# Gate products as seven block products for eight, with sums on GpSimd and additions on VectorE

## The reference

```python
h = x * (1 + sc1) + sh1
# three branches of attention: a (differential), b (neighbourhood), c (grouped queries)
ga, gb, gc = jnp.split(jax.nn.sigmoid(h @ w_gate_l + b_gate_l), N_BRANCH, axis=-1)
y = (ga * (oa @ w_br_l[0]) + gb * (ob @ w_br_l[1]) + gc * (oc @ w_br_l[2])) @ w_o_l
x = _layernorm(alpha * x + g1 * y, ln_g_l[0], ln_b_l[0])
h2 = x * (1.0 + sc2) + sh2
m = _moe(h2, w_router, router_bias, moe_w1_l, moe_w3_l, moe_w2_l)   # 16 experts, 2 taken
x = _layernorm(alpha * x + g2 * m, ln_g_l[1], ln_b_l[1])
```

## Time and profile before

| what | value |
| --- | --- |
| runs, us | 2165.38, 2165.5, 2169.61; median 2165.5 |
| span of the profiled execution, us | 2168.7 |
| PE busy, us | 2054.0 (95%) |
| DVE busy, us | 1131.9 (52%) |
| ACT busy, us | 508.2 (23%) |
| GpSimd busy, us | 196.2 (9%) |
| PE, products of 128x320, records of hT by ring | 2048, busy 604.0 us |
| mean granted clock of PE | 0.982 of full speed |

### The profile page before, as it was taken

The page is one execution under the profiler, slowest core; times in us unless marked ns, Lnnn a source line. Parts: engine busy times, 40 slices in busy tenths (PEclk is TensorE's granted clock), DMA queues, the critical chain, the costliest instruction groups (busy, mean ns, idle before and its releaser), DMA issues. The chain is left out here.

```text
span 2168.7 us, 25186 instructions
## 1 busy us (share of the span) xinstructions
PE 2054.0 (95%) x9738; PEld 1212.0 (56%) x9738; DVE 1131.9 (52%) x1782; ACT 508.2 (23%) x1007; POOL 196.2 (9%) x234
## 2 busy tenths in 40 slices
PE   7999999999999999699899999999999999969996
PEld 3457766576467654344244676656755676434432
DVE  1135458343447765756342453764534444866664
ACT  2014300242134400122130342003412342002221
POOL 1000010020110000100120002001101000010003
PEclk9999999999999999899999999999999999989997
DMA  7311146411122161689771112562111114238996
GB/s 303 129 47 39 37 144 237 138 54 44 39 81 98 68 278 75 252 342 359 265 256 39 63 35 69 199 214 86 47 53 49 42 40 172 91 136 313 382 350 186
DMA packets 62681, 317.01 MB, mean 146 GB/s; under 512 B 14824, under 2 KB 15280, under 8 KB 34272
## 3 DMA queue, kind: packets, MB, share of 16 engines
q1 hardware_dynamic: 32688, 232.41, 28.6%
q0 software_dynamic: 13136, 53.64, 7.6%
q10 hardware_dynamic: 16736, 29.32, 3.8%
HBM read 286.70 MB, written 27.07 MB: 145 GB/s over the span
## 5 line engine op out<-in xcount | busy, mean ns | idle before, releaser
L1081 PE MATMUL ps<-hT,ring 128*128 128x320 f32 x2048 | 604.0, 438 | 0.0
L1081 PEld LDWEIGHTS ps<-hT,ring 128*128 128x128 f32 x2048 | 369.7, 190 | 138.3 <-issue 3.3
L1081 PE MATMUL ps<-ring,hT 128*128 128x512 f32 (+1 forms) x960 | 386.6, 558 | 2.5 <-DVE hT L1995 1.7
L1081 PE MATMUL ps<-ring,zT 128*128 128x512 f32 (+2 forms) x992 | 317.6, 600 | 2.0 <-ACT zT L1898 2.0
L1081 PEld LDWEIGHTS ps<-ring,hT 128*128 128x128 f32 x960 | 178.8, 190 | 184.0 <-issue 174.8
L1081 PE MATMUL ps<-R,ring 128*128 128x512 f32 (+1 forms) x768 | 211.1, 435 | 4.6 <-DVE zT L2267 3.2
L1081 PEld LDWEIGHTS ps<-ring,zT 128*128 128x128 f32 (+2 forms) x992 | 121.5, 156 | 149.1 <-issue 146.3
L1830 ACT COPY R<-ps 128x512 f32<-128x512 f32 (+2 forms) x170 | 96.1, 565 | 374.7 <-PE ps L1330 372.5
L1081 PEld LDWEIGHTS ps<-R,ring 128*128 128x128 f32 x768 | 116.9, 191 | 99.3 <-issue 93.1
L2112 DVE SCALAR_TENSOR_TENSOR R<-ring,cs,R 128x2048 f32<-128x2048 f32 x56 | 131.7, 2352 | 5.5 <-DMA ring<-in_wall 3.5
L2193 DVE RECIPROCAL rinv<-rsum 128x2 f32<-128x2 f32 x96 | 15.9, 166 | 224.6 <-ACT R L1816 224.6
(11 more groups left out here) (302 smaller groups left out, 2045.7 us busy)
## 6 DMA issues: line engine op xcount, KB each, us to landing
ring<-in_wall SPq DMA_DIRECT2D x188, 1024.0 KB, 6.1
hT<-in_wall SPq DMA_DIRECT2D x20, 1024.0 KB, 8.5
y_all<-R ACTq DMA_DIRECT2D x27, 512.0 KB, 7.0
R<-in_wall SPq DMA_DIRECT2D x10, 1024.0 KB, 9.2
R<-in_rows POOLq DMA_DIRECT2D x2, 4096.0 KB, 15.7
R<-mrows POOLq DMA_DIRECT2D x16, 512.0 KB, 19.2
R<-in_x ACTq DMA_DIRECT2D x10, 512.0 KB, 9.5
h_rows<-R ACTq DMA_DIRECT2D x10, 512.0 KB, 2.6
```

Source lines behind the costliest of these rows:

```text
L1081: ins = nc.tensor.matmul(out, w, m, start=start, stop=stop, **kw)
```

## The change

A gate piece is now worked on as 2 x 2 blocks (`pair` p): rows low and high (four `k` each), columns first and second 128, by 2 x 2 blocks of tokens (low and high rows, early and late 320). Seven products of blocks (`LOW_LOW` to `HIGH_HIGH`), each of four 128x128x320 products (`STEPS`), take the place of eight. For this

- GpSimd makes sums of tokens (`token_sum`, 128 x 1280 columns, four a branch, of which branch 2 reuses three) and for each pair four sums of weights of 128x512 (`first_sums`, `last_sum`). The token sums of branch 0 lie in `SG`, those of branches 1 and 2 mostly in ring slots 4 and 5, so that only four slots hold weights there. The output weights ("o") wait for the last gate product.
- ACT copies the first product (`LOW_LOW`), takes tanh of the third straight from PSUM (`HIGH_LOW` is summed on top of `LOW_LOW`), and tanh of the other three quarters from `sg`.
- DVE makes six additions of 128x320 a pair into `sg` (`add_products`), called behind the maximum and behind the finish of each slot.
- PE waits for these at each product's first step.
- The slots have three steps ahead of the transpositions in place of four (branches 0 and 1), and a branch has 112 steps in place of 128. In branch 2 slots 1 to 16 have (3, 2) for (3, 3), slot 0 eight for four, and the tail 8 and 4 for 8 and 8.
- `masked_bias` of branch 1 is interleaved with the sums slot by slot.

The diff, cut to its core:

```diff
-TAIL_FILL = (8, 0, 8)
+TAIL_FILL = ((8,), (), (8, 4))
 UNIT_FILL = 2
 FILL = (
-    ((0, 6, 0),) + 6 * ((0, 4, 3),) + 4 * ((0, 4, 2),) + 6 * ((0, 4, 3),) + ((0, 6, 0),),
-    ((4, 6, 0),) + 16 * ((0, 4, 3),) + ((0, 6, 0),),
-    ((0, 4, 0),) + 16 * ((0, 3, 3),) + ((0, 4, 0),),
+    ((0, 6, 0),) + 12 * ((0, 3, 3),) + 4 * ((0, 3, 2),) + ((0, 6, 0),),
+    ((4, 6, 0),) + 16 * ((0, 3, 3),) + ((0, 6, 0),),
+    ((0, 8, 0),) + 16 * ((0, 3, 2),) + ((0, 4, 0),),
 )
...
+KEPT_SLOTS = (4, 5)
+TURNS = (2, 3, 0, 1)
...
+    w = j - len(PROJECT_SLOTS)
+    if w < 0:
+        at = PROJECT_SLOTS[j]
+    elif w < n:
+        at = TURNS[w % 4]
+    else:
+        at = (*KEPT_SLOTS, TURNS[n % 4], TURNS[(n + 1) % 4], TURNS[(n + 2) % 4], TURNS[(n + 3) % 4])[w - n]
...
+                        if what == ("o", 0, 0):
+                            sp.wait_ge(pe_gate, gate_no(2, PAIRS - 1, HIGH_HIGH))
                         load(i, lay, WALL.index(what))
...
+                    def first_sums(br, p):
+
+                        i, w = gate_piece(br, p)
+                        pool.wait_ge(full[slot_of(layer, i)], 16 * loads_by(layer, i))
+                        if br or p:
+                            pool.wait_ge(pe_gate, gate_no(br, p, LOW_LOW) - SEVEN + LATE)
+                        ch.step(nc.gpsimd.tensor_tensor(part_sum, w[:, low, 128:256], w[:, high, 128:256], ALU.add), g_sum)
+                        ch.step(nc.gpsimd.tensor_tensor(cross_sum[:], part_sum, w[:, low, 0:128], ALU.subtract), g_sum)
+                        ch.step(nc.gpsimd.tensor_tensor(w[:, low, 128:256], w[:, low, 0:128], w[:, low, 128:256], ALU.subtract), g_sum)
+
+                    def last_sum(br, p):
+
+                        i, w = gate_piece(br, p)
+                        pool.wait_ge(pe_gate, gate_no(br, p, CROSS))
+                        ch.step(nc.gpsimd.tensor_tensor(cross_sum[:], w[:, high, 0:128], cross_sum[:], ALU.subtract), g_sum)
...
+                            if c == 7:
+                                gate_sums(2, 0)
                             if c in (6, 7):
                                 for t in range(NT):
...
+                        for s in range(ITEMS + 2):
+                            if s:
+                                gate_sums(br, products_by(br, min(s, SLOT_COUNT) - 1, 2))
...
+                            if o == LOW_LOW:
+                                if k == 0:
+                                    if br or p:
+                                        pe.wait_ge(v_part, adds_by(br, p, LOW_LOW) - 1)
...
+                                weights, tokens = w[:, k, 0:128], hT[:, k, 0:320]
+                            elif o == CROSS:
+                                if k == 0:
+                                    if br or p:
+                                        pe.wait_ge(v_part, adds_by(br, p, LOW_LOW))
+                                    pe.wait_ge(g_sum, SUMS * (PAIRS * br + p) + 2)
+                                    pe.wait_ge(g_tok, sums_ready(br, 1))
+                                weights, tokens = cross_sum[:, k, :], token_row(layer, br, 1, k)
...
+                            elif o == DOWN:
+                                if k == 0:
+                                    pe.wait_ge(v_part, adds_by(br, p, CROSS))
...
+                            ins = mm(ps[:, 6 + (SEVEN * p + o) % 2, 0:320], weights, tokens, k == 0 and o != HIGH_LOW, k == STEPS - 1,
+                                     frees=k < STEPS - 1, skip_group_check=o in (LOW_LOW, HIGH_LOW))
...
+                            dve.wait_ge(pe_gate, gate_no(br, p, o))
+                            got = ps[:, 6 + (SEVEN * p + o) % 2, 0:320]
+                            first, second, third_, fourth = quarters(br, p)
+                            if o == CROSS:
+                                dve.wait_ge(a_low, PAIRS * br + p + 1)
+                                ch.step(V_.tensor_tensor(fourth, fourth, got, ALU.add), v_part)
+                            elif o == DOWN:
+                                ch.step(V_.tensor_tensor(third_, fourth, got, ALU.add), v_part)
+                            elif o == ACROSS:
+                                ch.step(V_.tensor_tensor(second, fourth, got, ALU.add), v_part)
+                                ch.step(V_.tensor_tensor(fourth, third_, got, ALU.add), v_part)
+                            elif o == LATE:
+                                ch.step(V_.tensor_tensor(second, second, got, ALU.add), v_part)
+                            else:
+                                ch.step(V_.tensor_tensor(third_, third_, got, ALU.subtract), v_part)
...
+                            if s == 0:
+                                add_products(br, fills(br)[0] // STEPS)
                             if s < ITEMS:
                                 maxima(br, s)
+                                if s:
+                                    add_products(br, products_by(br, s, 1))
...
                                 norm_output(done)
+                            if s < SLOT_COUNT:
+                                add_products(br, products_by(br, s, 2))
                             if br == 2 and not last_layer and 1 <= s < ITEMS:
                                 next_partials(s)
```

More of the change, by code:

```diff
@@ L219, in slot_of @@
         return SLOT_MOE[layer][i - MOE_FIRST[layer]]
[L220 to L225 removed]
+    return RING_ORDER[layer][place_in_ring(layer, i)]
 def summed_by_dve(layer, i):
@@ L961, in _ @@
                                     powers(small[:, 8:8 + nh], small[:, 0:nh])
+                            if c == 7:
+                                gate_sums(2, CROSS + 1)
+                            if c == 5:
+                                n = pieces.index((layer, ("in", 4, 1)))
+                                pool.wait_ge(freed, taken_by(layer, n)[1])
+                                for j in range(4):
+                                    token_sum(1, j)
+                                pool.wait_ge(mrow_out, 16 * 2 * STRIPS)
+                                gate_sums(1, 0)
                             i = PU.index((br, c, CTX))
@@ L1234, in project @@
                         done = len([q for q in QU if PU[q][0] <= br])
-                        for q in range(done - LAST_QK[br], done):
-                            fill(br, TAIL_FILL[br])
+                        for q, n in zip(range(done - LAST_QK[br], done), TAIL_FILL[br] or (0,) * LAST_QK[br]):
+                            fill(br, n)
                             transpose_unit(q)
@@ L1255, in fill @@
[L1255 to L1257 removed]
+                            p, step = divmod(filled[0] - PAIRS * SEVEN * STEPS * br, SEVEN * STEPS)
+                            o, k = divmod(step, STEPS)
+                            w = take("gate", ahead).rearrange("p (k n) -> p k n", k=8)
```

245 lines of the change are left out of this document (186 added, 59 removed).

## The result

The changed kernel takes 2174.9 us (median of 12 runs, 2167.3 to 2182.2), the kernel before 2169.2 (12 runs beside them). The ratio is 1.0029, with a 95% interval of 1.0016 to 1.0042: 0.3% slower, where 1.3% faster was forecast. The profiled execution's span is 2171.4 us, its mean granted clock 0.976 (0.982 before).

The account below looks back on a forecast made before the run. PE was taken as the bound nearly everywhere, VectorE level in branch 2, layer 0. Gains 9.8 + 14.0 + 6.5 - 1.8 - 1.0 = 27.5 us gave 2141.2, or 2138.0 on the median's scale; range 2130 to 2146, 8-in-10 2118 to 2157.

Parts of the forecast that it names:

- What bounds the kernel: Whole kernel: TensorE is busy 2054.0 of 2168.7 us; a removed step saves 0.54 us where PE sets the slot's length.
- Branch 0, slots 3, 7 and 11, waits of 0.9, 1.4, 0.9: Branch 0 attention: PE waits there for additions behind an output's norming, cutting a gain of 8.1 to 4.9 us a layer.
- rival B: GpSimd sums and VectorE hinder each other, in branch 2 of layer 0 and branch 0's outputs: about 2153 us; chance 0.20.
- Branch 1, slot 1, 1.07 later: Branch 1, slot 1: fourth product waits for an addition behind item 0's finish, 1.07 us later; branch net gain 7.0 a layer.
- Branch 2, slot 0 and 1: Branch 2, tail to slot 1, both layers: +2.1 for an addition behind the finish, -2.7 for five fewer steps; about 0.1 gained.
- Projection, chunk 6 to 7, 0.5 a layer: Branch 2 projection: weight sums delay GpSimd's power and chunk 7's unit, PE waits 0.4 to 0.5 us, 1.0 in both layers.
- Branch 2 of layer 0, 4.5 longer in its attention: Branch 2, layer 0: VectorE's 7.10 us loop lengthens; attention 116.3 us against 111.8 before, net 1.8 lost in the sum.
- The 2.6 us for additions behind the finish: Branch 2, layer 0: two additions in slot 4 and one each in slots 5, 9 and 13 lengthen VectorE's loop, 2.6 us.
- Ring of four, 0: Weight slots: two of six hold token sums, output weights wait; taken as 0, or 4 us lost if pieces came 5 later.
- A: Waits at product boundaries and VectorE's bound in layer 0 are smaller than worked out: gain 41, 2124.6 us; chance 0.15.
- C: VectorE's hand-over is late at every one of 168 products, PE waits 87 us: slower, 2201 us; chance 0.07.
- D: Weight pieces come late through the ring of four, 1.1 us for each of 24 gate pieces: 2165 us; chance 0.08.

Follow-up runs that it names:

- work in the wait: The changed kernel with two unused 128x320 products ahead of each of the three longest-waiting product starts, in both layers: 2161.3 us, ratio to before 0.9962.
- sums clear: The changed kernel with only GpSimd's order altered, sums waiting for VectorE's units at chunk 7 and output norming in branch 0: 2156.3 us, ratio 0.9943.
- idle sums: The kernel before the change with GpSimd making 96 sums of a scratch tile nobody reads, placed like the change's weight sums: 2180.3 us, ratio 1.0041.
- sums short: The changed kernel with GpSimd's sums cut to 4 columns of each block, waits, products and additions kept, output wrong: 2147.2 us.
- both orders: The changed kernel with VectorE's additions moved earlier and GpSimd's sums held until VectorE's unit or norming is done: 2138.8 us, ratio 0.9868.

## Why the prediction was wrong, point by point

- **What bounds the kernel**: right. PE sets the pace, and every plain slot fell by what was forecast.
- **Branch 0, slots 3, 7 and 11, waits of 0.9, 1.4, 0.9**: slots 7 and 11 were right (1.2 and 0.7), slot 3 failed: 2.83. The failed step is that the norming was taken at its length in the trace of before, 0.69 twice, though rival B had it listed as of the kind that collides. Two held-up operations are 1.9 us; the half speed behind them 1.7 and 3.0 more (11.55 and 12.76 against 9.8 with work in the wait, which has the same additions). Slot 15 holds the same collision with a pair's last sum (L2260 at 1.64, slot 7.17 for 6.25, and 6.29 with the sums clear). Together with a tenth each in slots 7 and 11 and 0.24 in slot 13 that is the shortfall of 11.6 in both layers.
- **Branch 1, slot 1, 1.07 later**: the mechanism and its size were right. The product waited for the addition behind the finish; shifted by the 1.33 us by which the branch started later, it started at 421.42 (422.75 less 1.33), and 420.83 + 0.52 = 421.35 was forecast. What failed is the end of the working: that behind the wait PE goes on at its pace. It ran at half speed, 1.5 and 1.8 us more. The rest of 6.1 is in slots 9, 10 and 13 (1.3 a layer).
- **Branch 2, slot 0 and 1**: the same step failed: behind the wait PE was taken to go on at its pace. The wait was there, 2.65 long, and the half speed behind it cost 1.6 to 1.7; the work beside a sum (L2420) another 0.36. In layer 1 this is the shortfall of 3.3, but for slots 6 and 7 (0.97, the output's copy behind the additions), which no term had.
- **Projection, chunk 6 to 7, 0.5 a layer**: mis-sized. I had the unit of chunk 7 late by its power. The unit of chunk 6 came first: its two operations were held up by 1.1 and 0.9, PE waited 3.82 in place of 1.79, and the clock fell. It cost 4.3 a layer. 3.7 of this the sums clear give back (121.25 to 117.55), and the idle sums show it apart from the change.
- **Branch 2 of layer 0, 4.5 longer in its attention**: 10.0 longer. 2.0 are the start, as above. The rest is slots 6, 7, 10 and 14 (9.91, 7.91, 8.98, 7.94). In slot 6 the output's copy stands behind two additions and a modulation sum that a sum of GpSimd holds up (3.10 for 2.35), PE waits 2.63 and goes on at half speed:

```profile
678.64 3.10 DVE L2366 SCALAR_TENSOR_TENSOR R<-ring,cs,R 128x2048 f32<-128x2048 f32 x1
679.67 3.20 POOL L1035 TENSOR_TENSOR cross_sum<-R,ring 128x512 f32<-128x512 f32 x1
684.65 2.02 PE L1550 MATMUL ps<-R 128*64 128x128 f32 x20 [2.63 <-DVE R L2459]
```

  VectorE works through its list in order; I counted the additions there and not who stands behind them. The 2.6 us for additions behind the finish were too much, for once: slot 5 has 1.05 of them, slots 4, 9 and 13 stay at 7.10.
- **Ring of four, 0**: right. The waits of PE name DMA of the ring for 3.0 us in the whole trace (1.9 before), 1.5 at most at once.
- **Rivals**: A and C were not the case (plain slots have no waits), D not. B was the right cause, in the wrong places and too small: I priced it in branch 2 of layer 0 and in branch 0's outputs, while it cost most at chunk 6 and at slot 3, and by the waits it lengthened and the clock behind them. Its range ended at 2160. The length of a sum was not what it missed: 1.27 us, where 1.45 was taken as the bound.

The trace of after settles the price that was open, in the timeline of slot 3 and in that of chunk 6: an operation of VectorE with both inputs in SBUF that meets a sum of GpSimd waits for the sum's end (0.69 becomes 1.63; L2260 ends 0.54 behind L1034), and an addition, with one operand in PSUM, does not (0.49 in all 26 cases). It also goes the other way: the sum L1035 beside the modulation sum took 3.20 for 1.27. The Trainium skill states just this ("SBUF — State Buffer", section "Who interferes with whom"), and the measurements agree. My fault was to give the rule a fifth of the chance and the sum none of its cost.

The share of each cause of the 33 us, as far as the runs separate them: about 13.6 are the half speed at the places where work was put into the wait and in slots 6 and 7; behind the wait at chunk 6 the clock adds about 1.4 more in layer 0 (16 records in 5.03 us that take 3.62 elsewhere), which I read from the rows and did not test apart. The places of the additions and the lock make the waits themselves; they overlap, 23 and 19 us if taken away alone, 36 together. What isn't separated is how much of these 19 is the time of the sums on GpSimd and how much the lock; the idle sums point to the lock, since nobody waited for them.

## What to carry to other kernels

When work is taken off the bounding engine and given to others in small pieces, price each piece by the queue that it stands in: who is behind it, and which operation of the neighbour it collides with. A sum of 1.27 us on GpSimd cost VectorE 0.9 to 1.1 us here for each operation of 128x512 with both operands in SBUF that met it whole; place it behind a signal that VectorE is done with those. Put an addition that the bounding engine needs where its own engine waits anyway; the same change went from 0.3% slower to 1.5% faster by order alone. And where TensorE waits, look at the granted clock of the records behind: the wait can cost more than its length.

## What was not expected of the hardware

- The same wait can go either way. In slot 10 of branch 2 in layer 0 PE waits 2.40 or 2.41 us in seven of these kernels: the slot takes 8.98 or 8.99 in five of them and 10.07 in two. The wait of 2.49 or 2.50 at the end of that branch was followed by eight records in 2.42 us in one kernel and in 3.65 in the next. With the sums short, slot 1 of branch 2 has a wait of 2.28 in both layers and takes 8.96 and 10.55. What decides it no run here shows. PE's timeline in slot 10, first with the sums clear (granted clock behind it 0.50), then with both orders (1.00):

```profile
708.37 2.40 PE L1558 MATMUL ps<-R 128*64 128x128 f32 x20 [2.40 <-DVE R L2467]
```

```profile
699.45 1.31 PE L1558 MATMUL ps<-R 128*64 128x128 f32 x20 [2.40 <-DVE R L2467]
```

- Work that nobody uses, put into a wait of PE, made the kernel 13.6 us faster (0.6%).
- With most of each addition left out the stretch with the experts of layer 0 takes 50 us longer, and the end of layer 1 51 to 103. Neither stretch has the additions in it: the time of this kernel depends on its data, most likely by the router, and a kernel that leaves part of the computation out must be compared by stages apart from the experts.
